# One block and one memory map for the state stages and the last projection of a two-layer model

## What is computed

```python
z, xbc, dt_raw, q, f_raw, i_in, g, u, s5_gate = jnp.split(proj, splits, axis=-1)
y_ssd = ssd_mixer(z, xbc, dt_raw, ...)        # chunked Mamba-2
y_hgrn = hgrn2_mixer(q, f_raw, i_in, g, ...)  # gated states, chunks of 32
y_s5 = s5_mixer(u, s5_gate, ...)              # complex diagonal states
mix = jnp.concatenate([y_ssd, y_hgrn, y_s5], axis=-1)
x = x + rms_norm_2(mix @ w_out[l], post_norm_w[l])
```

## Time and profile before

| what | us |
|---|---|
| median of three runs | 3331.94 |
| the profiled execution | 3326.63 |
| its span, first to last instruction | 3324.8 |
| gated states | about 2786 to 2944 |
| last instruction of the first Phase (SP's store) to first of the second | 2952.0 to 2955.2 |
| last mixer to the last gelu | 2955.2 to 3057.1 |
| glu, gates and projection | 3057.1 to 3324.8 |

### The profile page before, as it was taken

The page is one execution under the profiler, slowest core; times in us unless marked ns, Lnnn a source line. Parts: engine busy times, 40 slices in busy tenths (PEclk is TensorE's granted clock), DMA queues, the critical chain, the costliest instruction groups (busy, mean ns, idle before and its releaser), DMA issues. The chain is left out here.

```text
span 3324.8 us, 52663 instructions
## 1 busy us (share of the span) xinstructions
PE 2911.8 (88%) x21080; PEld 2505.4 (75%) x21080; DVE 1922.0 (58%) x2336; ACT 1279.9 (38%) x1816; POOL 764.2 (23%) x476
## 2 busy tenths in 40 slices
PE   8999996998576898599999959799999897966898
PEld 7999985877344787488888847699999865745687
DVE  4365644776365533798898845410068777667511
ACT  3000004554454331478878834211111166433411
POOL 3222212332171000222222101122322151222300
PEclk9999997998678998799999979899999988877999
DMA  5465322010411732799999953333466642042411
GB/s 185 152 216 199 117 86 91 31 32 13 87 44 68 287 116 87 286 393 400 405 399 393 397 187 127 141 112 128 154 205 214 203 181 102 23 159 52 146 68 48
DMA packets 193806, 559.76 MB, mean 168 GB/s; under 512 B 24720, under 2 KB 98576, under 8 KB 167456
## 3 DMA queue, kind: packets, MB, share of 16 engines
q1 hardware_dynamic: 147600, 459.71, 38.0%
q10 hardware_dynamic: 35632, 66.01, 5.5%
q0 software_dynamic: 10400, 31.65, 3.2%
HBM read 440.19 MB, written 124.32 MB: 170 GB/s over the span
## 5 line engine op out<-in xcount | busy, mean ns | idle before, releaser
L386 PE MATMUL pin_psum<-pin_sb_w,pin_sb_hT 128*128 128x354 f32 (+1 forms) x5376 | 975.0, 343 | 15.9 <-DVE pin_sb_hT L332 6.2
L386 PEld LDWEIGHTS pin_psum<-pin_sb_w,pin_sb_hT 128*128 128x128 f32 x5376 | 935.9, 189 | 52.5 <-DVE pin_sb_hT L332 6.9
L4316 DVE TENSOR_TENSOR moe_sb_wlo<-moe_sb_raw,moe_sb_whi 128x2048 fp32r<-128x2048 f32 x192 | 433.9, 2286 | 71.0 <-ACT moe_sb_whi L4128 71.0
L4128 ACT ACTIVATE moe_sb_whi<-moe_sb_raw 128x2048 fp32r<-128x2048 f32 x192 | 365.8, 1917 | 104.7 <-PE moe_psum L4391 75.5
L309 ACT ACTIVATE pin_sb_xt<-pin_psum,pin_sb_ss 128x353 f32<-128x353 f32 (+1 forms) x112 | 63.8, 589 | 564.4 <-PE pin_psum L386 493.9
L361 DVE TENSOR_SCALAR pin_sb_xt<-pin_psum,pin_sb_ss 128x353 f32<-128x353 f32 (+1 forms) x112 | 69.0, 625 | 330.7 <-PE pin_psum L386 330.5
L262 POOL CAST pin_sb_w<-pin_sb_raw 128x2832 fp32r<-128x2832 f32 (+1 forms) x26 | 75.3, 2898 | 627.9 <-PE pin_psum L386 583.1
L4391 PE MATMUL moe_psum<-moe_sb_whi,moe_sb_xhi 128*128 128x512 f32 x512 | 204.6, 400 | 8.6 <-DVE moe_sb_xlo L4320 8.6
L4391 PE MATMUL moe_psum<-moe_sb_whi,moe_sb_xlo 128*128 128x512 f32 x512 | 201.3, 393 | 0.0
L4391 PE MATMUL moe_psum<-moe_sb_wlo,moe_sb_xhi 128*128 128x512 f32 x512 | 201.0, 393 | 0.0
L264 POOL TENSOR_TENSOR pin_sb_w<-pin_sb_raw,pin_sb_w 128x2832 fp32r<-128x2832 f32 (+1 forms) x26 | 187.8, 7223 | 3.9 <-issue 0.7
(11 more groups left out here) (716 smaller groups left out, 5720.8 us busy)
## 6 DMA issues: line engine op xcount, KB each, us to landing
moe_sb_raw<-in_w_gate SPq DMA_DIRECT2D x64, 1024.0 KB
moe_sb_raw<-in_w_up SPq DMA_DIRECT2D x64, 1024.0 KB, 8.0
moe_sb_raw<-in_w_down SPq DMA_DIRECT2D x64, 1024.0 KB, 7.4
scratch_proj<-pin_sb_xt ACTq DMA_DIRECT2D x16, 1412.0 KB, 6.3
scratch_proj<-pin_sb_xt ACTq DMA_DIRECT2D x12, 1792.0 KB, 6.2
pin_sb_raw<-in_w_in SPq DMA_DIRECT2D x15, 1412.0 KB, 7.1
pin_sb_raw<-in_w_in SPq DMA_DIRECT2D x11, 1792.0 KB, 9.1
scratch_ybuf<-moe_sb_yb ACTq DMA_DIRECT2D x32, 512.0 KB, 8.3
```

The costliest lines, as they stand in the source:

```text
L386: mm = te.matmul(ps[:, t, 0:cols], hT[a_part][:, k, t * P:(t + 1) * P], wt[b][w_part][:, k, :], start=(k == 0 and n == 0), stop=(k == KD - ...
L4128: s.activation(whi[q][:, :, :], raw[q][:, :, :], ACT.Copy).then_inc(hi, 1)
L4316: tt(wlo[q][:, :, :], raw[q][:, :, :], whi[q][:, :, :].bitcast(F32), ALU.subtract).then_inc(lo, 1)
```

## The change

The two functions become one, state_mixes, with one Phase, one Block, one arena of 52864 words for each partition and one set of semaphores; the tiles of the last mixer are placed over tiles that are dead by then, small ones over dts. The names of the second part get an n_ where both had them (n_ident, n_states, n_y), UNITS becomes S5_UNITS. The shapes and the order of work outside of the lines below are those of before. The diff, cut to its core:

```diff
-        NORMS = ((9, (0, 1, 2, 3)), (15, (4, 5, 6)))
+        NORMS = ((9, HEAD_TILES),)
...
-        z_in = [ph.sem(f"z_in{t}") for t in range(NT)]
+        z_in = [ph.sem(f"z_in{i}") for i in range(3)]
+        z_group = lambda t: (t + 3) // 4
...
-                ve.wait_ge(z_in[t], 16)
+                ve.wait_ge(z_in[z_group(t)], (16, 64, 48)[z_group(t)])
```

SP, after the stores of the ssd tiles 4 to 7:

```diff
+            sp.wait_ge(y_st, 16 * NT)
+            sp.dma_start(n_ident[:, :], g["ident"]).then_inc(n_ident_in, 16)
+            (c_re and c_im into cn: 4 DMAs, before on GpSimd)
+            (uin; pw, bb, mag; bls; glub; n_nw: 7 DMAs)
+            for t in HEAD_TILES:
+                keep_gated(t)
+            sp.wait_ge(keyed, h_UNITS)
+            sp.wait_ge(scaled, h_UNITS)
+            (tab: 1 DMA)
+            sp.wait_ge(side, h_UNITS)
+            (d16: 1 DMA)
+            for t in TAIL_TILES:
+                keep_gated(t)
+            sp.wait_ge(h_y_st, 16 * NT)
+            sp.wait_ge(c_t, 1)
+            (glu_raw, then w_out slices 0 and 1, then as before)
```

(Lines in brackets stand for dma_start calls that are those of before but for their place.) GpSimd, before the memset of toep:

```diff
+            po.wait_ge(h_normed, NT)
+            po.wait_ge(final, h_UNITS)
```

ScalarE, after the last unit of the gated states:

```diff
-            keep(h_UNITS - 1)
-            h_roots((NT - 1,))
+            (c_t, then the 4 copies to cs)
+            keep(h_UNITS - 1)
+            (u_in, then the 4 copies to ug)
+            h_roots(TAIL_TILES)
+            (the copies to uc, blt and kern)
```

VectorE, after the last unit:

```diff
-            for t in NORMS[1][1]:
-                h_norm(t)
-            h_means((NT - 1,))
-            h_norm(NT - 1)
+            ve.wait_ge(pw_in, 48)
+            ve.wait_ge(c_c, 1)
+            ve.wait_ge(side, h_UNITS)
+            for h in range(4):
+                (the six instructions of ca on 4 of 16 columns of states, 128x576)
+                if h == 0:
+                    h_means(TAIL_TILES)
+            for t_ in TAIL_TILES:
+                h_norm(t_)
+            ve.wait_ge(final, h_UNITS)
```

TensorE, after the last unit; the kernel products wait for quarters of ca (ca_d, r + 1) in place of halves:

```diff
-            finish(h_UNITS - 1)
+            te.wait_ge(states, 2 * h_UNITS)
+            te.wait_ge(n_ident_in, 16)
+            te.wait_ge(c_in, 64)
+            (the 8 transposes of cn, into banks 6 and 7)
+            finish(h_UNITS - 1)
+            te.wait_ge(exps, h_UNITS)
+            te.wait_ge(clamped, h_UNITS)
```

More of the change, by code:

```diff
@@ new lines, in _, with load, keep @@
+            sp.dma_start(nw[:, :], g["ssd_norm_w_2"].partition_broadcast(P)).then_inc(nw_in, 16)
+            def load(dst, col, tiles, sem):
+                src = proj[tiles.start * P:tiles.stop * P, col:col + W].rearrange("(t p) c -> p t c", p=P)
+                sp.dma_start(dst, src).then_inc(sem, 16)
+            def keep(t):
+                sp.wait_ge(normed, t + 1)
+                sp.dma_start(y_ssd[t * P:(t + 1) * P, :], z[:, t, :]).then_inc(y_st, 16)
+            load(F[0][:, :, :], COL_F, BATCH[0], f_in[0])
@@ L3650, in _ @@
             tt, ts, stt = ve.tensor_tensor, ve.tensor_scalar, ve.scalar_tensor_tensor
[L3651 to L3653 removed]
+            acf = acum[:, :, :].rearrange("p t h -> p (t h)")
+            ve.memset(S[:, :, :], 0.0)
+            ve.memset(wide[:, :, :], 0.0)
+            ve.wait_ge(cum_p, 1)
@@ new lines, in carry @@
+            def carry(u, chunks):
+                t, q = h_units[u]
+                ve.wait_ge(outs, 2 * u + chunks[0] // 2 + 1)
+                if chunks[0] and u >= 2:
+                    ve.wait_ge(final, u - 1)
+                for c in chunks:
+                    ve.drain()
+                    for i in range(2):
+                        hs = slice(i * HD, (i + 1) * HD)
+                        ins = stt(h_S[q][:, (4 * t + c + 1) % RING, hs], h_S[q][:, (4 * t + c) % RING, hs],
+                                  dec[:, t, 2 * q + i, c:c + 1], ps[:, OUT + c % 2, hs], ALU.mult, ALU.add)
+                ins.then_inc(states, 1)
@@ new lines, in h_means, with h_norm @@
+            def h_means(tiles):
+                cut = slice(HH * tiles[0], HH * (tiles[-1] + 1))
+                ve.wait_ge(kept, GROUPS * (tiles[-1] + 1))
+                ts(h_ss[:, 1, cut], h_ss[:, 0, cut], 1.0 / HD, EPS, ALU.mult, ALU.add).then_inc(h_mean, len(tiles))
+            def h_norm(t):
+                ve.wait_ge(h_root, t + 1)
+                ve.wait_ge(gw_done, t + 1)
+                ve.reciprocal(h_ss[:, 3, HH * t:HH * (t + 1)], h_ss[:, 2, HH * t:HH * (t + 1)])
+                ve.drain()
+                for h in range(HH):
+                    hs = slice(h * HD, (h + 1) * HD)
+                    ins = stt(Q[:, t, hs], Q[:, t, hs], h_ss[:, 3, HH * t + h:HH * t + h + 1], G[:, t, hs], ALU.mult, ALU.mult)
+                ins.then_inc(h_normed, 1)
@@ new lines, in _ @@
+            for q in range(GROUPS):
+                ve.memset(at[q][:, :, :], 0.0)
+            ve.wait_ge(exps_a, 1)
+            score(0)
+            mask(0)
+            for u, (t, q) in enumerate(units):
+                if q == 1 and t + 1 < NT:
+                    score(t + 1)
+                if u + 1 < UNITS:
+                    mask(u + 1)
+                if u == UNITS - 1:
+                    gates(0)
+                join(u)
+                if u == 8:
+                    means(HEAD_TILES)
+                if 10 <= u < 10 + len(HEAD_TILES):
+                    norm(HEAD_TILES[u - 10])
@@ new lines, in _ @@
+            ve.wait_ge(prepared, NT)
+            for q in range(GROUPS):
+                ve.memset(h_S[q][:, 0, :], 0.0)
+            clamp(0)
+            decays(0)
+            means(TAIL_TILES)
+            ve.wait_ge(h_masks_in, 16)
+            for u in range(h_UNITS):
+                scale(u)
+                if u + 1 < h_UNITS:
+                    clamp(u + 1)
+                if u == 2:
+                    gates(1)
+                if u in (0, GROUPS * HEAD):
+                    ve.wait_ge(dec_a, batch_of(h_units[u][0]) + 1)
+                carry(u, (0, 1))
+                copy(u)
+                carry(u, (2, 3))
+                if u == 3:
+                    decays(1)
+                h_mask(u)
+                if 1 <= u < 1 + len(TAIL_TILES):
+                    norm(TAIL_TILES[u - 1])
+                for at_unit, tiles in NORMS:
+                    if u == at_unit:
+                        h_means(tiles)
+                    if at_unit < u <= at_unit + len(tiles):
+                        h_norm(tiles[u - at_unit - 1])
@@ new lines, in finish @@
+            def finish(u):
+                t, q = h_units[u]
+                te.wait_ge(h_masked, u + 1)
+                te.wait_ge(states, 2 * u + 2)
+                te.wait_ge(copy5, u + 1)
+                for i in range(2):
+                    hs = slice(i * HD, (i + 1) * HD)
+                    te.matmul(half(LAST, 1)[:, hs], at[q][:, i, :], V[:, t, HW * q + i * HD:HW * q + (i + 1) * HD],
+                              start=True, stop=False)
+                    for c in range(4):
+                        o = slice(32 * c, 32 * c + 32)
+                        mm = te.matmul(half(LAST, 1)[o, hs], T5[q][:, i, o], h_S[q][:, (4 * t + c) % RING, hs],
+                                       start=False, stop=True)
+                mm.then_inc(final, 1)
@@ new lines, in _ @@
+            turn(0)
+            score(0)
+            te.wait_ge(sel_in, 16)
+            te.wait_ge(aT_d, 1)
+            rows(0)
+            rows(1)
+            for u, (t, q) in enumerate(units):
+                if t + 1 < NT:
+                    turn(t + 1) if q == 0 else score(t + 1)
+                sums(u)
+                if u + 2 < UNITS:
+                    rows(u + 2)
+            te.wait_ge(h_masks_in, 16)
+            te.wait_ge(seg_a, UNITS)
+            sum_logs(0)
+            te.wait_ge(ind_in, 16)
```

1517 lines of the change are left out of this document (688 added, 829 removed).

## The result

The kernel after takes 3305.42 us (median of 17 runs, 3295.37 to 3313.57). The kernel before, by now also in 17 runs, takes 3324.55 (3307.81 to 3336.33), 7.4 less than the median of three on which the prediction stood. The ratio is 0.9942, with a 95% interval of 0.9931 to 0.9954: 19.1 us faster, by the interval 15.3 to 22.9. The second group of runs, on another chip, gives 3303.36 (6 runs) against 3326.38 (11), ratio 0.9935 (0.9912 to 0.9959).

A forecast was written before the change was run, and what follows sets the result against it. Waits in turn between the two Phases, no engine full, were taken to bound the kernel: 42.3 us of path. 17.7 sooner less 2.1 of GpSimd blocking gave 15.6, so 3316.3 us, range 3309 to 3323.

The forecast's parts named there:

- The seam: From the gated states' last h_mask to states(0): early loads and new order start states(0) 17.7 us sooner.
- the side of ug early: At states(0): ug's chain ready at 2964.0, before VectorE's norms end at 2968.75, so VectorE is last.
- GpSimd against VectorE: In the states: GpSimd's diagonal, add, glu_lo and memset block VectorE's SBUF pairs, adding 2.1 us in all.
- the queue falling into pieces: In the states: an addition of 0.2 us to the blocking of VectorE by GpSimd's work.
- The memset's 0.8: At the start of the states: the end of toep's memset on GpSimd blocks VectorE for 0.8 us.
- glu_lo (9.25) and the add ... stay: In the states: glu_lo blocks VectorE for 9.25 us and the add to kern for 1.07, as before.
- The base and the range: Whole kernel: 15.6 us off the three-run median 3331.94 gives 3316.3, range 3309 to 3323.
- The clock on outputs(3): Rival, chance 0.16: last output products run at the full clock, saving 4.1 us; with the memset free, 3311.4.
- Late glu_raw: Rival case, chance 0.13 with toep: glu_raw lands only at 2992 and delays the toep writes; up to 4.4 us lost.
- Late toep: Rival case, chance 0.13 with glu_raw: toep writes land at 3008, outputs(0) ends too late for gelu; 3320.7.
- No projection tile fell to the half clock: Rival, chance 0.04: one projection tile runs at TensorE's half clock, adding 21.8 us, 3338.
- the loads would not be early: Rival, chance 0.07: SP is held until unit 15 ends, so the transfers stay before states(0); no change, 3332.

The follow-up runs named there:

- no_tail_norms: Kernel after without the scaled products of the four tail tiles' norms, only reciprocals kept; h_mask of unit 15 to states(0) 22.12 us, against 25.63.
- norms_first: Kernel after with means and four tail norms ahead of ca instead of behind; h_mask of unit 15 to states(0) 29.25 us, against 25.63.
- after_again: Kernel after, unchanged, run again beside the kernel before; h_mask of unit 15 to the end 361.60 us, against 361.59.
- after_glu_dd: Kernel after with glu_lo on VectorE, d's load and diagonal ahead of the toep memset; 3297.33 us, ratio to the kernel before 0.9926.
- toep_first: Kernel of after_glu_dd with the toep writes ahead of the glu_raw and w_out loads; 3298.79 us, ratio to the kernel before 0.991.
- one_block: Kernel after with norms ahead of ca and loads only after the last store; h_mask of unit 15 to the end 379.16 us, against 361.59.
- late_loads: Kernel after with cn, uin and other loads back behind the last gated unit; h_mask of unit 15 to states(0) 38.32 us, against 25.63.
- late_loads_2: Kernel of late_loads with pw, bb and mag ahead of uin; h_mask of unit 15 to states(0) 35.79 us, against 38.32.
- after_glu_dve: Kernel after with glu_lo on VectorE ahead of the last gelu unit; h_mask of unit 15 to the end 358.15 us, against 361.59.
- glu_dve_toep: Kernel of after_glu_dve with the toep writes ahead of glu_raw and w_out; h_mask of unit 15 to the end 355.00 us, against 358.15.
- before_glu_dve: Kernel before with glu_lo on VectorE ahead of the last gelu unit; h_mask of unit 15 to the end 378.01 us, against 381.50.

## Why the prediction was right, and where it was wrong

**The seam: right.** ca 19.1 sooner relative to h_mask: 43.25 and 25.63 split into 21.81 and 2.73 ahead of ca's first instruction, 19.1. Quarters of 4.36: 2957.96 - 2953.60 = 4.36. Norms at a pitch of 1.30, VectorE last, the side of ug early: all shown, the last two by no_tail_norms. That side was ready 22.1 after the start of h_mask where 20.7 was reckoned, since the table load and the root (1.28 + 0.22), named but not added, do lie in it; it had 3.5 to spare. 17.7 was forecast and 17.6 came, and each term behind it as reckoned (ca starts 2.73 after h_mask for 2.65), so this is not luck.

**GpSimd against VectorE: wrong in sign.** The step "Added in all: 1.9, and 0.2 for the queue falling into pieces: 2.1" measured as 2.1 less. Three terms were off: the memset, the 0.2 for the queue falling into pieces, of which no run shows anything, and glu_lo. The memset's 0.8 was nothing (2970.79, 0.69, beside it; norms_first six times more). By the rule of the Trainium skill (SBUF — State Buffer, Who interferes with whom) it was to be nothing, and the traces agree. The diagonal and the add held: they cost the scans 2.0, about the 1.1 + 1.07 taken. And "glu_lo (9.25) and the add ... stay" was the real miss: I had glu_raw land earlier, but did not ask which VectorE instructions would then be above glu_lo. It started at 2979.40, 6.7 us after the start of the add where it was 1.8 in the kernel before, and four of VectorE's PSUM-input instructions (2982.39 to 2984.9) fell under it unhindered, 2.5 us; and where it was not caught right behind the add, VectorE got in between its pieces. So it cost 6.0 (5.8 in after_again) instead of about 9.25, and no instruction near 10 us came, which "What would show it" had named. That VectorE's time without stretches is the same in both kernels shows that no other term hides here: 67.84 - 7.29 - 10.1 = 50.4 and 65.72 - 7.29 - 8.0 = 50.4.

**The base and the range: wrong, and the larger part.** The forecast was 15.6 off 3331.94. Of the 10.9 us by which 3316.3 misses 3305.42, 7.4 are the base (3331.94 against 3324.55) and 3.5 the size of the gain; on the right base the same sum gives 3309.0. The step that failed is "with the 2 us that three runs lie around their median": three runs within 3.9 us say little when seventeen spread over 28.5. The profiled execution, 5.3 below that median, was a sign of it and was set aside. Part of the spread goes with the granted clock of the whole run: of the 29 runs of the kernel before beside after_again, after_glu_dd and toep_first, the six at 0.917 or 0.918 took 3327.6 to 3331.9 and the three at 0.922 3316.7 to 3318.5, but two at 0.923 took 3328.6 and 3328.7. The rest of it stays open.

**The rivals.** The clock on outputs(3) did not change: its products, 1.22 each from 3023.41 on, are on the path in the kernel after. What it would give was seen in norms_first, where its last three groups of eight ran at the full clock, and in one_block, where four did: VectorE's last wait is 5.81 and 5.29 for 7.29, so 0.5 a group, and 4.1 for all eight was priced rightly. Late glu_raw: it landed about 7.4 after its issue (2970.81 to ScalarE's start at 2978.27), under 10 as argued. Late toep: outputs(0) came 24.7 after states(0) (2992.30 for 2967.64) where 23.2 was forecast (2992 for 2968.85), since the writes took 16.36 of issue for 13.3; it was not on the path. But "ten us to spare" was too much. ScalarE had VectorE's first gel ready 4.7 us early (3001.64 + 1.09 against 3007.43), and TensorE paused 3.4 ahead of outputs(3); take 6 us from VectorE, and it is the bound. No projection tile fell to the half clock: from the last gelu unit to the end it took 270.24 for 270.41. That the loads would not be early is refuted by their rows at 2858.

## What to carry to other kernels

Price a move of loads or work across a seam from a fixed instruction just ahead of it to the next one that all wait for; that number repeated to 0.02 us here where the whole program moved by ten; a sum up to the end, with 270 us of other work in it, only to 1 or 2 us. Price GpSimd's reading instructions by what VectorE executes at that very moment (two SBUF inputs or a scan stand still, a PSUM input does not), and expect a shift of either to change it; better, put such work where VectorE waits anyway. Before taking more from one engine, look at how early the next one is, and at which clock.

## What the runs showed beyond the expectation

A VectorE instruction caught by glu_lo stood for all four of its pieces where these ran in a row behind the add to kern (10.83 in the kernel before, 11.01 in norms_first, 10.99 in one_block), but for only about one piece at a time (2.88, 2.40, 2.83) where glu_lo began on its own, in after_again, late_loads, late_loads_2 and no_tail_norms too. In the kernel after the pieces themselves lengthened, from 2.33 to between 2.35 and 2.79, as if both sides took turns. Why a series begun on its own lets VectorE in was not tried and stays open.

The eight toep writes took 15.3 to 16.9 us of issue right behind the 3 MB of glu_raw and w_out (after, after_again, after_glu_dve, after_glu_dd, late_loads), 12.7 and 13.2 ahead of them (toep_first, glu_dve_toep), and 13.1 to 13.9 where those loads had been issued about 7 us or more before (the kernel before, before_glu_dve, norms_first, one_block, no_tail_norms, late_loads_2).

The same stretching is left in the gates of both kernels. VectorE's product of the two halves of hg (L3766 before, 128x512, both inputs in SBUF) takes 0.69 at best, but three of its eight take 2.46 to 2.48 in each kernel, in the kernel before from 3081.17 on, with GpSimd's difference for w_out beside them. Whether these 5 us are on the path was not tried.
